# The variance sums of a hybrid decoder step: a third halving of the squares on VectorE and one product with a matrix of ones in place of two

## The reference

```python
DEEPNORM_ALPHA = (2.0 * DEPTH) ** 0.25          # DEPTH = 2

def layer_norm(x, g, b):
    xf = x.astype(jnp.float32)
    mu = jnp.mean(xf, axis=-1, keepdims=True)
    var = jnp.mean(jnp.square(xf - mu), axis=-1, keepdims=True)
    return ((xf - mu) * lax.rsqrt(var + LN_EPS) * g + b).astype(x.dtype)

for i in range(DEPTH):                           # i = 0: attention, i = 1: retention
    mp = mixer(xp)                               # ends in a product with w_o
    xp = layer_norm(DEEPNORM_ALPHA * xp + mp, ln_mix_g[i], ln_mix_b[i])
    fp = conv_ffn(xp, ...)                       # up, causal conv of width 3, silu, gate, down
    xp = layer_norm(DEEPNORM_ALPHA * xp + fp, ln_ffn_g[i], ln_ffn_b[i])
```

## Time and profile before

| | us |
|---|---|
| median of 3 runs | 2875.41 (2874.73 to 2875.43) |
| the profiled execution | 2874.99 |
| its span, first to last instruction | 2873.1 |
| PE busy | 2815.1 (98% of the span) |
| DVE busy | 1482.7 (52%) |
| ACT busy | 906.4 (32%) |
| POOL busy | 597.1 (21%) |
| mean granted clock of TensorE | 0.993 of full speed |

### The profile page before, as it was taken

The page is one execution under the profiler, slowest core; times in us unless marked ns, Lnnn a source line. Parts: engine busy times, 40 slices in busy tenths (PEclk is TensorE's granted clock), DMA queues, the critical chain, the costliest instruction groups (busy, mean ns, idle before and its releaser), DMA issues.

```text
span 2873.1 us, 44770 instructions
## 1 busy us (share of the span) xinstructions
PE 2815.1 (98%) x18372; PEld 2709.0 (94%) x18372; DVE 1482.7 (52%) x2974; ACT 906.4 (32%) x1690; POOL 597.1 (21%) x505
## 2 busy tenths in 40 slices
PE   8999989999999999999999999999999999999996
PEld 7888879999999999999999999899999999999996
DVE  6555576444444444614445454465775444444446
ACT  5445454221111122422443433422252221222223
POOL 3334351000000002402223232122330000000004
PEclk9999999999999999999999999999999999999998
DMA  4210011111111112235666566775412111111101
GB/s 134 79 46 17 30 46 45 45 45 45 52 52 45 45 45 65 68 116 150 185 187 195 184 189 184 237 253 190 139 30 74 45 45 57 47 45 45 45 26 59
DMA packets 193436, 260.53 MB, mean 91 GB/s; under 512 B 29201, under 2 KB 151697, under 8 KB 193201
## 3 DMA queue, kind: packets, MB, share of 16 engines
q1 hardware_dynamic: 128336, 196.16, 22.0%
q10 hardware_dynamic: 64896, 61.50, 6.3%
HBM read 191.50 MB, written 68.20 MB: 90 GB/s over the span
## 4 chain that ended last, share of the span: by engine, by line
PE 92%; DVE 4%; ACT 2%; issue 1%; POOL 1%; DMA 0%; SPq 0%; ACTq 0%; DVEq 0%; POOLq 0%
PE bank L493 29%; PE bank L495 28%; PE bank L494 28%; PE bank L628 1%; ACT y L1045 1%; PE bank L650 1%; PE bank L954 1%; PE bank L917 1%; PE bank L640 1%; DVE bank L1524 0%; PE bank L902 0%; PE bank L605 0%; ACT xh L1049 0%; PE bank L546 0%; DVE y L1531 0%
## 5 line engine op out<-in xcount | busy, mean ns | idle before, releaser
L493 PE MATMUL bank<-xh,wh 128*128 128x344 f32 x3600 | 1159.6, 322 | 4.8 <-DVE wl L1477 2.9
L495 PE MATMUL bank<-xh,wl 128*128 128x344 f32 x3600 | 1149.6, 319 | 0.0
L494 PE MATMUL bank<-xl,wh 128*128 128x344 f32 x3600 | 1149.0, 319 | 0.0
L493 PEld LDWEIGHTS bank<-xh,wh 128*128 128x128 f32 x3600 | 676.5, 188 | 20.3 <-issue 9.4
L494 PEld LDWEIGHTS bank<-xl,wh 128*128 128x128 f32 x3600 | 675.9, 188 | 4.9
L495 PEld LDWEIGHTS bank<-xh,wl 128*128 128x128 f32 x3600 | 676.5, 188 | 0.0
L1502 DVE TENSOR_TENSOR y<-bank,y 128x344 f32<-128x344 f32 x576 | 289.7, 513 | 218.7 <-PE bank L495 217.9
L2155 POOL TENSOR_TENSOR f_hl<-f_cv,f_hh 128x344 fp32r<-128x344 f32 x132 | 123.2, 934 | 1265.2 <-ACT f_hh L1197 1265.2
L493 PE MATMUL bank<-f_hh,wh 128*128 128x344 f32 x1056 | 339.8, 322 | 0.0
L495 PE MATMUL bank<-f_hh,wl 128*128 128x344 f32 x1056 | 337.3, 319 | 0.0
L494 PE MATMUL bank<-f_hl,wh 128*128 128x344 f32 x1056 | 337.1, 319 | 0.0
(11 more groups left out here) (234 smaller groups left out, 3491.3 us busy)
## 6 DMA issues: line engine op xcount, KB each, us to landing
raw<-in_w SPq DMA_DIRECT2D x216, 512.0 KB, 3.7
scratch_qkvg<-p_plain ACTq DMA_DIRECT2D x96, 172.0 KB, 2.9
r_s<-in_state_in SPq DMA_DIRECT2D x32, 512.0 KB, 3.8
out_state_s<-r_s ACTq DMA_DIRECT2D x32, 512.0 KB, 5.3
scratch_qkvg<-p_rot ACTq DMA_DIRECT2D x24, 344.0 KB, 3.8
xh<-scratch_heads_hi SPq DMA_DIRECT2D x12, 688.0 KB, 8.5
xl<-scratch_heads_lo SPq DMA_DIRECT2D x12, 688.0 KB, 9.4
r_cxq<-scratch_qkvg SPq DMA_DIRECT2D x32, 256.0 KB, 5.7
```

The costliest lines, as they stand in the source:

```text
L493: pe.matmul(out, ah, bh, start=(k == 0), stop=False)
L494: pe.matmul(out, ah, bl, start=False, stop=False)
L495: mm = pe.matmul(out, al, bh, start=False, stop=(k == n - 1))
```

## The change

`sum2` gets a third add, of tile 1 onto tile 0 (344 elements in each partition), after a wait for the second one. The second add now raises `n_half`, which therefore counts two for each chunk, and the third raises `n_sum2`. `var` multiplies one tile with the ones where it multiplied two. In the special code for u = 11 only the count that the wait on `n_half` compares with changes, from 12 + half to 23 + half.

```diff
@@ var(u), PE
-        for k in range(2):
-            mm = pe.matmul(b[:, 0:CH], K.ones[:, :], K.sq[:, k, :], start=(k == 0), stop=(k == 1))
-        mm.then_inc(S["n_var"], 1)
+        pe.matmul(b[:, 0:CH], K.ones[:, :], K.sq[:, 0, :], start=True, stop=True).then_inc(S["n_var"], 1)
@@ sum2(u), DVE
         dve.wait_ge(S["n_sq"], u + 1)
         dve.tensor_tensor(sq[:, 0:4, :], sq[:, 0:4, :], sq[:, 4:8, :], ALU.add).then_inc(S["n_half"], 1)
-        dve.wait_ge(S["n_half"], u + 1)
-        dve.tensor_tensor(sq[:, 0:2, :], sq[:, 0:2, :], sq[:, 2:4, :], ALU.add).then_inc(S["n_sum2"], 1)
+        dve.wait_ge(S["n_half"], 2 * u + 1)
+        dve.tensor_tensor(sq[:, 0:2, :], sq[:, 0:2, :], sq[:, 2:4, :], ALU.add).then_inc(S["n_half"], 1)
+        dve.wait_ge(S["n_half"], 2 * u + 2)
+        dve.tensor_tensor(sq[:, 0, :], sq[:, 0, :], sq[:, 1, :], ALU.add).then_inc(S["n_sum2"], 1)
@@ the last chunk, DVE
-        dve.wait_ge(S["n_half"], 12 + half)
+        dve.wait_ge(S["n_half"], 23 + half)
```

## The result

| | before | after |
|---|---|---|
| median, us (20 runs each) | 2874.59 (2870.92 to 2876.51) | 2878.07 (2873.15 to 2881.11) |
| ratio, 95% interval | | 1.0013 (1.0007 to 1.0019) |
| profiled execution, us | 2874.99 | 2880.75 |
| span, us | 2873.1 | 2878.9 |

The change costs 3.5 us, between 2.0 and 5.5. The forecast was +3.6 (2879.0 against 2875.4).

A forecast was written before the change was run, and what follows sets the result against it. PE, busy 98% of the span, was taken as the bound, with chains over ACT, DVE and POOL where it waits. Terms summed to +3.7 us on the profiled 2874.99, plus 0.42 to the median: 2879.0 us, range 2874.3 to 2880.3.

The forecast's parts named there:

- `n_sum2(0)` later: At u = 0 the third add waits for POOL's split of a slab, so its result comes 2.57 us later.
- u = 0 on the chain: 2.57 us later, 1.2 back from the shorter product: root, reciprocal, scaling and adds, and so PE, shift by +1.4 us.
- `n_sum2(1)` later, beyond that: At u = 1 the third add waits for POOL's split, so its result comes 2.59 us later.
- low clock at `var(1)`: After 3.6 us idle PE runs u = 1's product at the 1.2 GHz level: +2.6 us, +2.0 at the high level.
- u = 0 to 2, to the low part of chunk 2: Shift of PE from u = 0 through u = 2: 1.4, 2.6 and 0.55 us, +4.55 in all.
- u = 4, 7, each: POOL blocks the third add, but 2.7 us of slack hide it, so PE gains the saved product: -0.58 us each.
- u = 8, to the low part of chunk 8: Third add free but the chain late, behind a PE wait of 1.16 us: +0.55 us.
- the prediction's sign of being wrong: Waits for the low part at chunks 5 and 8 should grow 0.5 to 1.7 us; wrong if PE waits nowhere longer.
- The case of one blocked add: Rival: only one of the third adds at u = 0 and 1 is blocked: 2875.9 or 2877.1 us; chance 0.10.
- the third add isn't blocked: Rival: at u = 0 and 1 DVE keeps its turn; sum -0.95 us, 2874.5; chance 0.17.
- POOL keeps its turn through two splits: Rival: at u = 1 both POOL splits run before the third add; sum 6.4 us, 2881.8; chance 0.10.
- All products gained: Rival: the third add is hidden everywhere, so every removed product is gained: 7.0 us off, 2868.4; chance 0.03.

The follow-up runs named there:

- e2: Kernel before with only the second product removed, two halvings kept, tile 1 of the squares left out: 2869.93 against 2874.68 us, ratio 0.9984.
- c1: Kernel before, unchanged, run once more for a second profile: 2875.20 us.
- c2: Changed kernel, unchanged, run once more: 2877.87 against 2873.32 us for the kernel before, ratio 1.0014.
- e1: Changed kernel, but the third add writes to a tile nothing reads and PE keeps both products: 2886.16 against 2874.68 us, ratio 1.0043.
- e3: Changed kernel with POOL waiting for the third add before one split each at u = 0 and 1: 2873.70 against 2874.68 us, ratio 0.9997.
- e7: Changed kernel plus a fourth, unread add at u = 1 behind its own wait: 2881.39 against 2874.57 us, ratio 1.0024.
- e8: Kernel before with the change at u = 0, 4, 7, 10 only, POOL's split 23 held behind u = 0's third add: 2873.77 against 2873.32 us.
- e4: Kernel before with the change for u = 2 to 10 only: 2876.07 against 2874.68 us, ratio 1.0008.

## Why the prediction was right

The forecast's mechanism held, and the measured 3.5 us are close to its 3.6, in part by luck (*The sum*, below). The shifts of PE's starts in the changed kernel's first profile, less the 0.22 us at the start, give each term:

| step | forecast, us | profile, us |
|---|---|---|
| `n_sum2(0)` later | 2.57 | 2.59 |
| u = 0 on the chain | +1.4 | +1.7 |
| `n_sum2(1)` later, beyond that | 2.59 | 2.57 |
| low clock at `var(1)` | yes | yes (1.51 us for one product) |
| u = 0 to 2, to the low part of chunk 2 | +4.55 | +4.9 |
| u = 3, 6, 9, each | 0 | -0.02 |
| u = 4, 7, each | -0.58 | -0.57, -0.56 |
| u = 4 and 5 together | -0.33 | -0.38 |
| u = 8, to the low part of chunk 8 | +0.55 | +0.54 |
| u = 10 | -0.45 | -0.42 |

- *The third add.* Free 0.52 us (forecast 0.51 and a wait of 0.04), behind a POOL add 1.13 (1.17), behind a split 2.54 (2.5). It fell at each u as forecast. Not every DVE instruction is held up so: in the kernel before, a residual add, which has one input in PSUM, took 0.52 us at 375.11, inside POOL's split of 374.74 to 377.12.
- *u = 0* was 0.3 us too small. The product did get 1.15 us shorter (1.51 for 2.66), but DVE's reciprocal started only 0.9 earlier for it: behind the third add, a residual add now waited for a product that PE ran at the low clock, and it let the reciprocal start 0.26 us later than the root did. That is the term that was mis-sized. The idle times ahead of `var` were off too: 4.09 us at u = 0 and 4.19 at u = 1, where 4.8 and 3.6 were expected, because the clock was low at other times than in the profile before (0.50 from 388.5 to 391 us, 1.00 before), so that PE came to its waits later or earlier.
- *u = 2, 5 and 8.* That saved products are lost ahead of a chain is shown by e2, where the three waits grow without any third add, and by the changed kernel at u = 2 (0.37 us for 0.2) and 8 (1.73 for 1.16). At chunk 5 its wait is shorter (0.71 for 0.90), against the prediction's sign of being wrong, which wanted it 0.5 to 1.7 longer: PE had already idled for 0.69 us ahead of `var(5)`. The shift there is still as forecast.
- *The sum.* The terms of the profile make about +4.1 us (5.5 at the last chunk, less 0.22 at the start, less 1.15 of scatter), the forecast's 3.7; the medians say 3.5 and 4.5. Their intervals (2.0 to 5.5, 1.4 to 6.6) hold both sums, and the executions differ by more than that (last section). The sum was built on one order of turns at u = 0, and there is a second, which the forecast didn't know. From the mean product of u = 0 to that of u = 3 the change cost 4.97 us in the first pair of profiles (forecast 4.55), but 2.88 in the pair of c1 and c2, which have the second order. The medians are over executions of an unknown mix of both, so that they come within 0.2 us of the forecast is partly luck.
- *The rivals.* The case of one blocked add was added up wrong in one of its two prices: with the add blocked at u = 0 alone the sum is 3.7 - 2.6 = 1.1, so 2876.5 and not 2875.9. That the third add isn't blocked is wrong (2.54 us, e1, e3); that POOL keeps its turn through two splits is wrong (the changed kernel's rows and e7). All products gained is wrong by e2's profile. e3 shows the rule by removing what it needs: with the two splits out of the way the loss was gone.

The Trainium skill's rule on the shared port pair (SBUF - State Buffer, section "SBUF: two separate sides") agrees with these rows in that one instruction has the port and the other is fully blocked (2.54 us for an add that takes 0.52). The rows add who comes next: of two instructions, the one that was waiting when the other ended, also against the other engine's next instruction. That holds where DVE's instruction waits for a semaphore of the one before it and is issued 0.04 us behind its end, as every third add is. L2063 goes the other way: what it waits for was there already, it was issued 0.08 us before the end of the instruction ahead of it, and it went before a POOL instruction that was waiting. That the semaphore makes the difference was argued in the prediction; no run varied it.

## What to carry to other kernels

An add that halves what a product has to sum is to be priced with the turn that it gives away: it costs its own length only if the other engine on the port isn't running or waiting, and otherwise what is left of that engine's instruction as well (2.54 us against 0.52 here). So read the timeline of the other engine at the moment at which the new instruction would ask, and hold back its long instructions there if they aren't urgent. And where a chain over other engines ends last (u = 2, 5, 8 here), work taken off the busiest engine turns into wait.

## What the runs showed of the hardware that wasn't expected

**Two orders at one place.** The twelve profiles (both kernels twice, e1 to e8) show two orders of turns at u = 0, decided before the third add is reached. In eight of them the first halving lasts 1.77 to 2.26 us because one of POOL's adds is already running, in four (c1, c2, e2, e3) 1.58. DVE, POOL and PE in c1, the kernel before:

```profile
386.85 1.58 DVE L1517 TENSOR_TENSOR n_sq<-n_sq 128x1376 f32<-128x1376 f32 x1
386.88 2.32 POOL L2141 TENSOR_TENSOR n_ms<-n_ms,y 128x344 f32<-128x344 f32 x1
389.98 2.66 PE L546 MATMUL bank<-n_sq,ones 128*128 128x344 f32 x4 [1.73 <-DVE n_sq L1519]
```

DVE's first halving was issued 0.03 us ahead of POOL's add and took 1.58 us. In the first profile of the same program POOL had the port, the halving took 2.12, and `var(0)` began 1.14 us later relative to the mean product before it. In the order of c1 POOL's split comes later, so the third add meets only one of its adds: in c2, the changed kernel,

```profile
389.50 1.10 DVE L1519 TENSOR_TENSOR n_sq<-n_sq 128x344 f32<-128x344 f32 x1
```

it lasted 1.10 us instead of 2.54. So which order an execution has is worth 1.1 us in the kernel before and 1.4 us of a blocked add in the changed one. The lead of DVE is small (0.01 to 0.03 us in the four profiles), but the order isn't decided there: POOL's sums come later in c1, since the split ahead of them starts at 381.34 us, and at 379.97 in the first profile. It goes with TensorE's clock. The stretch from 370 to 372 us in the first profile of before and then in c1; the number third from the end is the granted clock:

```profile
370.00:372.00 2.00, 0.29 (x3) 0.13 (x2) 1.75 (x6) 1.98 (x4) 1.71 (x3) 1.00 0.00 0
```

```profile
370.00:372.00 2.00, 0.44 (x4) 0.25 (x3) 1.72 (x6) 2.00 (x4) 1.69 (x2) 0.50 0.00 0
```

It is 0.50 there in the four profiles of the second order and 1.00 in the other eight. What makes it fall in the one execution and not in the other is not shown. The runs of the changed kernel lie 8 us apart; this is one part of it, and no run here tells how large a part.

**The clock after the same idle time.** Ahead of `var(1)` the unchanged code idled for 1.02 us in the first profile of before and for 1.76 in e4 and c1; behind it the granted clock stayed at full speed in before and c1 and fell to the 1.2 GHz level in e4. PE at `var(1)` in c1 and in e4, both with two products:

```profile
413.33 1.42 PE L546 MATMUL bank<-n_sq,ones 128*128 128x344 f32 x4 [1.76 <-DVE n_sq L1519]
```

```profile
415.17 2.48 PE L555 MATMUL bank<-n_sq,ones 128*128 128x344 f32 x4 [1.76 <-DVE n_sq L1528]
```

The same idle time had both outcomes, worth 1.6 us in PE's next starts. So it was at 1860 us: behind 2.88 us of idleness the clock stayed up in the profile before, and behind 2.54 it fell in that of the changed kernel.
